# Two attentions' values computed as columns, two heads side by side, with the softmax shares multiplied into the probabilities

## What is computed

```python
z = rms(x) @ w_in                       # queries, keys, values and gates of three mixers
# banded attention: 8 heads of 64, 2 key/value heads, a window, a sink per head
p = exp(s - m);  p = p / (sum(p) + exp(sink - m));  ya = p @ v
# forgetting attention: 4 heads, causal, decay between query and key
p = softmax(s + F_q - F_k);                         yb = p @ v
# mLSTM: 4 heads, gated; its output is normed per head and gated
yc = sigmoid(co) * rms_head(mlstm(...))
x = x + concat(ya, yb, yc) @ w_out
x = x + square(relu(rms(x) @ w_ff1)) @ w_ff2
```

## Time and profile before

| | us |
|---|---|
| median of three runs | 1755.48 (1753.43 to 1758.86) |
| the profiled execution: its time | 1753.97 |
| the profiled execution: span, first to last instruction | 1752.7 |
| PE busy | 1630.1 (93%) |
| PE weight loads busy (beside PE) | 1252.6 (71%) |
| DVE busy | 821.2 (47%) |
| ACT busy | 670.5 (38%) |
| POOL busy | 31.3 (2%) |
| mean granted clock of PE, share of full | 0.974 |

### The profile page before, as it was taken

The page is one execution under the profiler, slowest core; times in us unless marked ns, Lnnn a source line. Parts: engine busy times, 40 slices in busy tenths (PEclk is TensorE's granted clock), DMA queues, the critical chain, the costliest instruction groups (busy, mean ns, idle before and its releaser), DMA issues. The chain is left out here.

```text
span 1752.7 us, 22969 instructions
## 1 busy us (share of the span) xinstructions
PE 1630.1 (93%) x9636; PEld 1252.6 (71%) x9636; DVE 821.2 (47%) x1428; ACT 670.5 (38%) x1035; POOL 31.3 (2%) x53
## 2 busy tenths in 40 slices
PE   6999999999888999999899989899999989989999
PEld 5788997444334788899643433778899977879998
DVE  6666566210005568556411001764555548455554
ACT  5354543111103344544211111664544445634443
POOL 5000000000000000000000000000000000000000
PEclk9999999999999999999999999998999999799999
DMA  9443358699997443255779999422455534225552
GB/s 309 155 145 120 131 206 330 270 367 421 419 383 294 150 156 140 84 209 224 321 304 416 421 419 418 152 94 82 144 186 190 193 121 145 97 98 191 192 184 105
DMA packets 58404, 393.75 MB, mean 225 GB/s; under 512 B 7436, under 2 KB 7452, under 8 KB 14124
## 3 DMA queue, kind: packets, MB, share of 16 engines
q1 hardware_dynamic: 55008, 381.35, 56.9%
q0 software_dynamic: 3136, 9.50, 1.8%
q10 hardware_dynamic: 144, 1.30, 0.2%
HBM read 391.07 MB, written 1.05 MB: 224 GB/s over the span
## 5 line engine op out<-in xcount | busy, mean ns | idle before, releaser
L1713 DVE TENSOR_TENSOR ring_rounded<-ring_sb,ring_rounded 128x2048 fp32r<-128x2048 f32 (+3 forms) x180 | 386.0, 2155 | 259.4 <-ACT ring_rounded L1325 259.2
L1325 ACT ACTIVATE ring_rounded<-ring_sb 128x2048 fp32r<-128x2048 f32 (+3 forms) x180 | 322.5, 1804 | 194.9 <-PE psum L604 178.7
L604 PE MATMUL psum<-ring_sb,region_sb 128*64 128x512 f32 x1440 | 335.3, 604 | 31.5 <-DMA ring_sb<-in_weights 20.0
L604 PE MATMUL psum<-xT_hi_rounded,ring_rounded 128*128 128x256 f32 x1920 | 350.8, 284 | 0.0
L604 PEld LDWEIGHTS psum<-xT_hi_rounded,ring_rounded 128*128 128x128 f32 x1920 | 301.4, 193 | 0.6
L604 PE MATMUL psum<-ring_rounded,region_rounded 128*128 128x512 f32 x1184 | 286.0, 391 | 4.1 <-DVE region_rounded L2414 2.1
L604 PE MATMUL psum<-xT_lo_rounded,ring_rounded 128*128 128x256 f32 x960 | 275.5, 287 | 5.8 <-DVE xT_lo_rounded L2156 5.8
L604 PEld LDWEIGHTS psum<-ring_sb,region_sb 128*64 128x64 f32 x1440 | 107.5, 139 | 235.7 <-issue 233.5
L604 PEld LDWEIGHTS psum<-ring_rounded,region_rounded 128*128 128x128 f32 x1184 | 221.0, 188 | 51.7 <-DVE region_rounded L2414 2.6
L604 PE MATMUL psum<-ring_rounded,xT_hi_rounded 128*128 128x512 f32 (+4 forms) x832 | 235.8, 362 | 20.4 <-DVE ring_rounded L1713 13.0
L604 PEld LDWEIGHTS psum<-xT_lo_rounded,ring_rounded 128*128 128x128 f32 x960 | 185.5, 193 | 8.7 <-DVE xT_lo_rounded L2156 6.2
(11 more groups left out here) (266 smaller groups left out, 1303.0 us busy)
## 6 DMA issues: line engine op xcount, KB each, us to landing
ring_sb<-in_weights SPq DMA_DIRECT2D x328, 1024.0 KB, 6.9
ring_sb<-in_weights SPq DMA_DIRECT2D x16, 768.0 KB, 4.3
region_sb<-in_weights SPq DMA_DIRECT2D x6, 1024.0 KB, 10.4
ring_sb<-in_weights SPq DMA_DIRECT2D x8, 584.0 KB, 10.5
ring_sb<-in_weights SPq DMA_DIRECT2D x4, 536.0 KB, 4.7
region_sb<-in_mem_turned POOLq DMA_DIRECT2D x2, 1024.0 KB, 7.2
region_sb<-in_pool_band POOLq DMA_DIRECT2D x2, 1024.0 KB, 8.0
region_sb<-in_ln_g POOLq DMA_DIRECT2D x4, 512.0 KB, 5.1
```

The lines of the kernel that those rows point to most:

```text
L604: return nc.tensor.matmul(dst, lhsT, rhs, start=first, stop=last, skip_group_check=True)
L1325: nc.scalar.activation(rounded(piece.hi), piece.raw, ACT.Copy).then_inc(hi_made, 1)
L1713: nc.vector.tensor_tensor(rounded(piece.raw), piece.raw, reread(piece.hi), ALU.subtract).then_inc(lo_made, 1)
```

## The change

Values of the banded and the forgetting attention are computed with the roles swapped: the head's values (128 keys by 64) are the loaded weights and the transposed probabilities are streamed, 128 columns. The result has the head's 64 channels as rows and queries as columns, which is the form that `yT` needs, so it needs no transpose. Heads 2c and 2c+1 go to the two halves of the 128 PSUM partitions, alternating. As queries are now columns, the division by the sums moves: DVE multiplies the reciprocals (of the sum, or of sum and sink) into the block's probabilities, by one instruction with broadcast, before PE transposes them. The transposes wait for that (`swa_shared`, `fox_shared`) where they waited for the exponentials. The bank of the banded values is read by `act_y` and `lower_y` directly. The forgetting values of a block go into the first half of the bank whose second half takes the two remaining transposes, those of the mLSTM rows. The orders of PE, ACT and DVE change with it.

```diff
+        mls["rows"] = shaped(xT[1].rearrange("p c t -> p (c t)")[:, 0:TB * 256], TB, 256)
...
+        def pe_pairs(i, c, b, probsT, values):
+
+            for kb in range(b + 1):
+                for odd in range(2):
+                    last = matmul(psum[odd * HD:(odd + 1) * HD, i, c * P:(c + 1) * P], values(2 * c + odd, kb),
+                                  probsT[:, 2 * c + odd, kb * P:(kb + 1) * P], kb == 0, kb == b)
+            return last
+
         def pe_swa_values(l, b):
-            pe_value_rows(("swa_out", l, b), b, SWA_HEADS, swa["probsT"], lambda h, kb: z2[:, kb, C2_AV + h // 4 * HD:C2_AV + (h // 4 + 1) * HD],
-                          swa_turned.at(l, 1 if b == 0 else 5), swa_y.at(l, b))
+            i, free, full = loose.take(("yT", l, 0, b), y_lo.at(l, b))
+            pe.wait_ge(*swa_turned.at(l, 1 if b == 0 else 5))
+            pe.wait_ge(*free)
+            for c in range(SWA_HEADS // 2):
+                last = pe_pairs(i, c, b, swa["probsT"], lambda h, kb: z2[:, kb, C2_AV + h // 4 * HD:C2_AV + (h // 4 + 1) * HD])
+            last.then_inc(full, 1)
 
         def pe_fox_values(l, b):
-            pe_value_rows(("fox_out", l, b), b, FOX_HEADS, fox["probsT"][:, 0:4, :] if b else fox["probsT"][:, 4:6, :].rearrange(
-                "p h (k n) -> p (h k) n", k=2), lambda h, kb: z2[:, kb, C2_BV + h * HD:C2_BV + (h + 1) * HD],
-                fox_turned.at(l, 0 if b == 0 else 2), fox_y.at(l, b))
+            i, free, _ = loose.take(("yT", l, 1, b), y_lo.at(l, 2 + b))
+            pe.wait_ge(*fox_turned.at(l, 0 if b == 0 else 2))
+            pe.wait_ge(*free)
+            probsT = fox["probsT"][:, 0:4, :] if b else fox["probsT"][:, 4:6, :].rearrange("p h (k n) -> p (h k) n", k=2)
+            for c in range(FOX_HEADS // 2):
+                pe_pairs(i, c, b, probsT, lambda h, kb: z2[:, kb, C2_BV + h * HD:C2_BV + (h + 1) * HD])
 
...
-        def pe_turn_y(l, part_, b):
-            i, free, full = loose.take(("yT", l, part_, b), y_lo.at(l, 2 * part_ + b))
-            pe.wait_ge(*(mls_y.at(l) if part_ else swa_y.at(l, b)))
-            pe.wait_ge(*free)
-            for c in range(4):
-                last = nc.tensor.transpose(psum[:, i, c * P:(c + 1) * P], y_rows[part_][:, b, c * P:(c + 1) * P], ident)
+        def pe_turn_y(l, b):
+
+            i, (full, _) = loose.of(("yT", l, 1, b))
+            pe.wait_ge(*mls_y.at(l))
+            for c in range(2):
+                last = nc.tensor.transpose(psum[:, i, (2 + c) * P:(3 + c) * P], mls["rows"][:, b, c * P:(c + 1) * P], ident)
             last.then_inc(full, 1)
...
             def swa_probs(b):
                 pe_turn_probs(("swa_probs", l, b), swa["probs"][b], SWA_HEADS, b + 1, [swa_turned.at(l, 2 * b + n) for n in range(2 * b + 2)],
-                              swa_exped.at(l, b * 8 + 7))
+                              swa_shared.at(l, b))
 
             def fox_probs(b):
                 pe_turn_probs(("fox_probs", l, b), fox["probs"][b], FOX_HEADS, b + 1, [fox_turned.at(l, b + n) for n in range(b + 1)],
-                              fox_exped.at(l, b * 4 + 3))
+                              fox_shared.at(l, b))
...
             pe_swa_values(l, 0)
             cut(5, lambda: swa_probs(1))
             pe_fox_scores(l, 1)
-            pe_swa_values(l, 1)
             pe_mls_scores(l, 0)
             pe_mls_scores(l, 1)
+            pe_swa_values(l, 1)
             fox_probs(0)
-            pe_turn_y(l, 0, 0)
+            mls_probs(0)
             fox_probs(1)
-            pe_turn_y(l, 0, 1)
-            mls_probs(0)
-            pe_fox_values(l, 0)
             mls_probs(1)
             pe_attended(l, 0, 0)
-            pe_fox_values(l, 1)
             pe_mls_values(l, 0)
             pe_mls_values(l, 1)
             pe_attended(l, 0, 1)
-            pe_turn_y(l, 1, 0)
-            pe_turn_y(l, 1, 1)
+            for b in range(TB):
+                pe_fox_values(l, b)
+            for b in range(TB):
+                pe_turn_y(l, b)
             pe_attended(l, 1, 0)
             pe_attended(l, 1, 1)
...
             act_exps(fox["probs"][0], FOX_HEADS, P, softmax_stats("fox", 0, FOX_HEADS), fox_lowered.at(l, 0), 1.0, fox_exped)
+            act_y(l, 0, 0)
             act_probs(("swa_probs", l, 1), SWA_HEADS, 2, swa_room, swa_turned)
             cut(5)
             act_mls_weights(l, 1)
             act_exps(fox["probs"][1], FOX_HEADS, S, softmax_stats("fox", 1, FOX_HEADS), fox_lowered.at(l, 1), 1.0, fox_exped)
+            act_y(l, 0, 1)
             act_probs(("fox_probs", l, 0), FOX_HEADS, 1, pair_room(fox, 0), fox_turned)
-            act_y(l, 0, 0)
+            act_probs(("mls_probs", l, 0), MLSTM_HEADS, 1, pair_room(mls, 0), mls_turned)
             act_probs(("fox_probs", l, 1), FOX_HEADS, 2, pair_room(fox, 1), fox_turned)
-            act_y(l, 0, 1)
-            act_probs(("mls_probs", l, 0), MLSTM_HEADS, 1, pair_room(mls, 0), mls_turned)
             act_probs(("mls_probs", l, 1), MLSTM_HEADS, 2, pair_room(mls, 1), mls_turned)
...
-            def swa_values(b):
+            def shares(name, b, heads, sums, probs_, shared):
+
+                keys = (b + 1) * P
+                nc.vector.reciprocal(sums, sums).then_inc(*vs.next())
+                vs.settle()
+                nc.vector.tensor_tensor(probs_[:, :, 0:keys], probs_[:, :, 0:keys], sums.unsqueeze(2).to_broadcast([P, heads, keys]),
+                                        ALU.mult).then_inc(shared.sem, 1)
+
+            def swa_shares(b):
                 _, sums = softmax_stats("swa", b, SWA_HEADS)
                 v.wait_ge(*swa_exped.at(l, b * 8 + 7))
                 v.wait_ge(*sink_exped.at(l, b))
                 nc.vector.tensor_tensor(sums, sums, stat(f"swa_extra{b}", SWA_HEADS), ALU.add).then_inc(*vs.next())
                 vs.settle()
-                nc.vector.reciprocal(sums, sums).then_inc(*vs.next())
-                vs.settle()
-                divided(y_rows[0][:, b, :], ("swa_out", l, b), SWA_HEADS, sums, swa_y)
-
-            def fox_values(b):
-                _, sums = softmax_stats("fox", b, FOX_HEADS)
+                shares("swa", b, SWA_HEADS, sums, swa["probs"][b], swa_shared)
+
+            def fox_shares(b):
                 v.wait_ge(*fox_exped.at(l, b * 4 + 3))
-                nc.vector.reciprocal(sums, sums).then_inc(*vs.next())
-                vs.settle()
-                divided(y_rows[1][:, b, 0:256], ("fox_out", l, b), FOX_HEADS, sums, fox_y)
+                shares("fox", b, FOX_HEADS, softmax_stats("fox", b, FOX_HEADS)[1], fox["probs"][b], fox_shared)
...
             swa_scores(0)
             decay_rows()
             swa_scores(1)
+            swa_shares(0)
             round_lo(first + 13)
             mls_gates(0)
             fox_scores(0)
             mls_gates(1)
-            swa_values(0)
+            swa_shares(1)
             mls_gain()
+            lower_y(0, 0)
             round_lo(first + 15)
+            fox_shares(0)
             fox_scores(1)
-            swa_values(1)
             mls_scores(0)
             mls_scores(1)
-            lower_y(0, 0)
+            fox_shares(1)
             lower_y(0, 1)
             round_lo(first + 16)
-            fox_values(0)
-            fox_values(1)
             mls_values()
             for b in range(TB):
                 lower_y(1, b)
```

More of the change, by code:

```diff
@@ L442, in build_program @@
         mls = dict(probs=[early(12 * P, 4, P), early(16 * P, 4, S)], squares=early(24 * P, TB, 256))
-        queries_at = cut[0]
         swa.update(qT=part(4, S), kT=part(2, S), probs=[part(8, P), part(8, S)], probsT=part(8, S))
@@ L447, in build_program @@
         key_rows, key_minus = part(S)[0:16, :], early(12 * P, S)[0:16, :]
-        y_rows = [shaped(region[:, queries_at:queries_at + TB * BANK], TB, BANK),
-                  shaped(xT[1].rearrange("p c t -> p (c t)")[:, 0:TB * BANK], TB, BANK)]
+        mls["rows"] = shaped(xT[1].rearrange("p c t -> p (c t)")[:, 0:TB * 256], TB, 256)
         squares = shaped(region[:, 0:TB * D], TB, D)
@@ L571, in build_program @@
             signal(n, c) for n, c in (("swa_summed", 1), ("swa_rooted", 1), ("swa_roped", 1), ("swa_qk_made", 3)))
-        swa_scored, swa_lowered, swa_exped, sink_exped, swa_turned, swa_y = (
+        swa_scored, swa_lowered, swa_exped, sink_exped, swa_turned, swa_shared = (
             signal_after(n, c) for n, c in ((dsa_scored, 16), (dsa_lowered, 2), (dsa_exped, 16), (mv_made, 2),
-                                            (dsa_turned, 6), (dsa_out, 2)))
+                                            (dsa_turned, 6), (dsa_shared, 2)))
         sink_lowered = signal("sink_lowered", 2)
@@ L579, in build_program @@
             signal(n, c) for n, c in (("fox_gained", 1), ("fox_summed", 1), ("fox_rooted", 1), ("fox_normed", 1), ("fox_qk_made", 2)))
-        fox_scored, fox_lowered, fox_exped, fox_turned, fox_y = (
-            signal_after(n, c) for n, c in ((mem_scored, 8), (mem_lowered, 2), (mem_exped, 8), (mem_turned, 3), (mem_out, 2)))
```

(6 more changed lines are left out.)

## The result

The changed kernel takes 1733.33 us (median of four runs, 1731.23 to 1737.13), the kernel before 1754.74 us with one more run of it: a ratio of 0.9879, 95% interval 0.9857 to 0.9901. The forecast was 1748.0 us, with a range from 1741 to 1755. The direction was right, the size was not: 21.4 us where 7.5 were forecast. Later, on another chip, the changed kernel had 1733.23 us and a ratio of 0.9901 (0.9875 to 0.9926).

What follows compares the result with a forecast made beforehand. PE's own instructions were taken to bound the touched stretch, mostly at half clock. Same-clock gains of 5.8 us plus 1.7 us for one shorter stretch gave 7.5 us less: 1748.0 us, range 1741 to 1755.

Steps and rivals of the forecast that it cites:

- same clock: Both layers' touched steps with no extra shortening of half-clock stretches: 0.6 + 2.7 and 0.6 + 1.9, together 5.8 us gained.
- the least for it: Last forgetting score to output product: at full clock DVE's shares come 0.9 us late, making 8.0 us the minimum.
- (b): Value records: column halves don't overlap for 128 columns, 0.112 us a record; no change, 1755.5 us; chance 0.15.
- (d): Value records: loads not hidden behind the other half's stream, up to 0.25 us a record; 1761 to 1775 us; chance 0.06.
- 0.165 us a record: Value records priced by the skill's load rule and load figure, making the kernel some 7 us slower.
- The step that failed: Half-clock stretches, two per layer: one of the four taken as 3.4 us shorter, worth 1.7 us.
- the first step: Before the last input projection's end: banded values at half clock fall from 3.4 to 2.2 us, worth 0.6 us a layer.
- the second step: Last forgetting score to output product: 10.9 us against 13.6 in the first layer, 12.6 against 14.5 in the second.
- Rival (a): Both steps: clock hardly falls, or rises early everywhere; gains 16.9 us, 1738.6 us, half of it 1743 to 1745; chance 0.20.
- The shares at nothing: DVE's multiplications of reciprocals into probabilities: some 3.2 us more on DVE, costed at nothing because covered by other work.

Runs made afterwards that it cites:

- e3: Changed kernel with both heads of a pair written to the lower 64 PSUM rows, so value records cannot overlap; 1742.88 us, ratio 0.9949.
- e15: Changed kernel run again unchanged, on another chip with more executions, for a second trace; 1732.65 us.
- e2: Changed kernel with the old order: second block's banded values ahead of the mLSTM scores, transposes in the old sequence, forgetting values still late; 1747.04 us, ratio 0.9970.
- e5: Kernel before, with the first block's banded values moved behind the first half of the last input projection, nothing removed; 1752.22 us, ratio 1.0000.
- e7: Changed kernel with one rounding of weights on DVE moved from ahead of the first mLSTM gates to the next group of roundings; 1733.25 us, ratio 0.9883.
- e10: Kernel of e2 without the four DVE multiplications of the shares, division left out of the result; 1739.88 us, ratio 0.9930.
- e12: Changed kernel with both e7's moved rounding and e8's key-block order; 1731.71 us, ratio 0.9885.
- e1: Kernel before with order alone changed: both mLSTM scores ahead of the second block's banded values, on PE and DVE; 1750.31 us, ratio 0.9986.
- e6: Kernel before with the shares alone: DVE multiplies them into the probabilities, values stay by rows and are only copied out; 1759.37 us, ratio 1.0040.
- e11: Changed kernel with value records alone put back to rows form (load 128 columns, stream 64), new order kept; 1748.01 us, ratio 0.9967.
- e13: Kernel of e11 run again unchanged for a second trace; its profiled execution took 1741.99 us.
- e14: Kernel of e11 run a third time unchanged for another trace; its profiled execution took 1738.34 us.
- e9: Changed kernel without the four DVE multiplications of the shares, division left out of the result; 1735.28 us, ratio 0.9910.
- e8: Changed kernel with the even head's key blocks first, then the odd head's, instead of alternating records; 1732.38 us, ratio 0.9898.
- e4: Changed kernel with the twelve transposes a layer put back as idle copies; 1736.32 us, ratio 0.9908.

## Why the prediction was wrong, point by point

**The work was near.** Count each stretch at half clock as half its length. Half clock makes up 92.2 us of the trace before and 64.8 of the one after, 27.4 us less, worth 13.7 us. The spans differ by 19.4 us, which leaves 5.7 us of work and waits; the sum for "same clock" said 5.8. That this pair comes so close is in part luck: within its two layers work and waits are 7.3 us (15.8 less 8.5 of clock), and over all executions they are 8.7. The records cost 0.061 us at full clock and 0.119 at half clock, for 0.068 and 0.136. The step from the last forgetting score to the output product took 8.6 us, and the least for it was put at 8.0, from DVE's queue. At no load or overlap did rivals (b) and (d) show. The Trainium skill says (TensorE: Matmul & The Clock Gate, part 3) that loads overlap with running products only in another row group; for these column halves this case speaks against it. All records here use the same rows. By that sentence the prediction estimated 0.165 us a record; measured were 0.107 us in one half (e3) and 0.061 us in two, where a pair takes 0.122 us.

**The step that failed** is "I take one of the four stretches as shorter by 3.4 us, 1.7 us of gain". All four were shorter, by 17 us together, worth 8.5 us, and three falls of 3.4 us at the norms' gaps, which the sum did not hold at all, were missing in the trace after, worth 4.4 us. That is 12.9 us of clock in this pair, and 9.2 us over all executions, where 1.7 were taken.

What the runs put in its place, for the first step: the work right behind the gates has a part in when half clock ends. With column-form values or dense products there, the stretch was 6.8 us or less in all 22 layers traced (the changed kernel and e15, e2 to e5, e7 to e10, e12). With rows-form values there it was 10.2 us in 11 of 12 (before, e1, e6, e11, e13, e14); the exception is e6's first layer. This I had as a reason, and gave it one stretch of four.

For the second step the runs do not show that. e11, e13 and e14, with rows form in the new order, had no half clock there in six layers, where the changed kernel had 3.4 us in each. The same instructions had 6.8 and 10.2 us in the two layers before, and order alone (e1) gave none and 10.2. What shortened this step's stretches is open. The prediction also says that before each rise of the clock PE did dense products or a run of transposes. At the rise of 1203.5 us in the first layer that is not so; values in rows form and mLSTM scores stood before it, and the transposes began behind it:

```profile
1203.63 0.66 PE L759 MATMUL psum<-consts_sb,region_sb 128*128 128x128 f32 x4
```

**Rival (a)** came nearest. It had 16.9 us for the two layers, and 15.8 were measured. Its mechanism holds by half: the clock still fell in every step, and rose early in each. It got a chance of 0.20, its extreme of 1738.6 us lay outside the range, and the falls at the norms' gaps are in no rival.

**The shares at nothing** held in the new order (e9) and fails in the old (e6, 7 us slower). I costed the shares against the covers of the new order and treated the order as something that costs or saves nothing by itself. In fact order alone gives 1 us (e1), columns with shares in the old order 4.5 us (e2), and both together 18 to 21. The order is what keeps DVE's shares off PE's path.

**What stays open.** What made the clock fall less, beyond the first step. On average 78 us at half clock were left of 85 with rows form in the new order, and 67 in the changed kernel, and no trace says in which stretches the long executions differ. Whether the three falls at the gaps go because of the change, or by where they happen to lie: they are absent in all traces of the changed kernel, e8, e11, e13 and e14, but one to three of them are present in e3, e4, e7, e9, e10 and e12, which are near to it. And e1's gain is not to be told from nothing.

## What to carry to other kernels

A stretch where TensorE runs at half clock should be priced with both levels and with its length left open, since what is scheduled into it can set its length; here records that load more than they stream went with the longer stretch right behind the gates. Moving them away shortened that stretch and gained no time (e5), so such a move has to be measured to the end. In this kernel's f32, a product of 128 x 64 with 64 columns was worth turning round, so that it loads 64 and streams 128 in two column halves: 0.061 us for 0.105, and the transposes behind it go. When an edit moves a division ahead of a transpose, reorder the engines so that something independent stands between; here the shares cost 7 us where nothing did (e6, and e2 against e10), and nothing that could be measured where something did (e9).

## What the runs showed of the hardware beyond that

Two layers with the same work, in one execution, differed by 4.6 us (e1), with 10.2 us more at half clock in one, and the executions of one kernel by 13 us (e11), with 59 to 91 us at half clock. One trace is then no measure of such a stage: the clock of all executions has to be looked at. Records that load 64 columns and stream 128 ran 0.061 us apart when they alternated between the two column halves, about as close when they changed halves only at every second record (24 in 1.58 us against 1.53), and 0.107 us apart in one half.
